# A slot earlier for the gates of the first recurrence, and its freed slot inside the tail of that recurrence

## The reference

```
h = rmsnorm(x, norm_mix_pre)
proj = h @ w_in                      # gq gk gv gg1 gr | pu | mq mk mv | gates
logit = gg1 @ w_g2 + b_g             # the recurrence's gate
log_a = log_sigmoid(logit) / 16
bc = cumsum(log_a) over time         # chunked in the reference, one scan in the kernel
attn[t,s] = sum_d q[t,d] k[s,d] exp(bc[t,d]-bc[s,d]),  s <= t
o = attn @ v ;  o = rmsnorm(o) * norm_w * silu(r)        # -> branch a
yb = pool_mixer(pu) ; yc = moba_mixer(mq, mk, mv)        # moba: 8 heads of causal softmax attention
mixed = s0 * (ya @ Wa) + s1 * (yb @ Wb) + s2 * (yc @ Wc) ; x = x + rmsnorm(mixed @ w_out)
```

## Time and profile before

| | before |
|---|---|
| median of 3 runs | 1155.04 us (1150.1 to 1155.22) |
| the profiled execution | 1149.21 us |
| its span, first to last instruction | 1147.0 us |
| mean granted PE clock in it | 0.996 |
| PE / ACT / DVE busy | 97% / 53% / 65% |

### The profile page before, as it was taken

How to read it: one execution, slowest core, us unless ns; L and a number is a source line. 1 busy time by engine, 2 the same in 40 slices (tenths; PEclk the granted TensorE clock), 3 DMA queues, 4 the chain that set the end, 5 groups by cost and what they waited for, 6 DMA issues and landing times.

```text
span 1147.0 us, 22790 instructions
## 1 busy us (share of the span) xinstructions
PE 1108.8 (97%) x9528; PEld 1053.9 (92%) x9528; DVE 750.1 (65%) x975; ACT 608.0 (53%) x788; POOL 0.2 (0%) x4
## 2 busy tenths in 40 slices
PE   7999999999999999999999999979999999999997
PEld 7999999989999998999999999979998989999997
DVE  6355667676555555688879565665557666777776
ACT  5364555346444444677566544366454546554554
POOL 0000000000000000000000000000000000000000
PEclk9999999999999999999999999999999999999999
DMA  7533435454555454344434434333444554555540
GB/s 261 215 109 114 149 146 185 177 189 158 184 184 185 183 187 177 111 147 153 180 111 152 147 145 147 110 112 131 164 150 149 209 191 151 186 197 183 183 183 37
DMA packets 27111, 184.40 MB, mean 161 GB/s; under 512 B 3080, under 2 KB 3608, under 8 KB 5400
## 3 DMA queue, kind: packets, MB, share of 16 engines
q1 hardware_dynamic: 26456, 181.38, 43.8%
q10 hardware_dynamic: 576, 1.85, 0.5%
HBM read 182.17 MB, written 1.05 MB: 160 GB/s over the span
## 4 chain that ended last, share of the span: by engine, by line
PE 78%; DVE 11%; ACT 8%; issue 2%; DMA 0%; ACTq 0%; SPq 0%; DVEq 0%
PE pp L303 55%; DVE wlo L285 5%; ACT whi L278 4%; PE pm L1653 3%; PE pm L1654 3%; PE pm L1655 3%; PE pm L883 1%; PE pm L384 1%; PE pm L386 1%; PE pm L385 1%; PE pm L757 1%; ACT XH L732 1%; PE pm L723 1%; PE pm L891 1%; PE pm L1502 1%
## 5 line engine op out<-in xcount | busy, mean ns | idle before, releaser
L285 DVE TENSOR_TENSOR wlo<-raw,whi 128x2048 fp32r<-128x2048 f32 x169 | 386.4, 2291 | 215.0 <-ACT whi L278 210.9
L303 PE MATMUL pp<-XH,whi 128*128 128x256 f32 x1696 | 485.7, 286 | 7.6 <-DVE wlo L285 6.1
L303 PE MATMUL pp<-XL,whi 128*128 128x256 f32 x1696 | 480.5, 283 | 0.0
L303 PE MATMUL pp<-XH,wlo 128*128 128x256 f32 x1696 | 480.5, 283 | 0.0
L278 ACT ACTIVATE whi<-raw 128x2048 fp32r<-128x2048 f32 x169 | 321.6, 1909 | 48.8 <-PE pp L303 31.7
L303 PEld LDWEIGHTS pp<-XH,whi 128*128 128x128 f32 x1696 | 325.8, 192 | 14.7 <-issue 7.8
L303 PEld LDWEIGHTS pp<-XL,whi 128*128 128x128 f32 x1696 | 325.9, 192 | 0.8
L303 PEld LDWEIGHTS pp<-XH,wlo 128*128 128x128 f32 x1696 | 325.8, 192 | 0.0
L1707 ACT ACTIVATE Y<-P 128x256 fp32r<-128x256 f32 x44 | 18.4, 418 | 132.6 <-DVE P L1740 132.6
L303 PE MATMUL pp<-Y,whi 128*128 128x256 f32 x480 | 86.9, 283 | 0.0
L303 PEld LDWEIGHTS pp<-Y,whi 128*128 128x128 f32 x480 | 75.2, 192 | 0.0
(11 more groups left out here) (308 smaller groups left out, 1303.3 us busy)
## 6 DMA issues: line engine op xcount, KB each, us to landing
raw<-stream SPq DMA_DIRECT2D x169, 1024.0 KB, 4.8
P<-gains ACTq DMA_DIRECT2D x3, 512.0 KB, 3.5
X<-xt SPq DMA_DIRECT2D x2, 512.0 KB, 4.4
raw<-stream SPq DMA_DIRECT2D x2, 512.0 KB, 6.8
out<-P SPq DMA_DIRECT2D x4, 256.0 KB, 2.2
C<-consts SPq DMA_DIRECT2D x1, 345.5 KB, 11.6
P<-rows_w ACTq DMA_DIRECT2D x1, 272.0 KB, 2.7
U<-poolw SPq DMA_DIRECT2D x1, 256.0 KB, 10.5
```

The source lines that it names most:

```text
L285: dve.tensor_tensor(wlo[:, slot, :], raw[:, slot, :], whi[:, slot, :].bitcast(F32), ALU.subtract).then_inc(lo_ready, 1)
L303: done = pe.matmul(dst, a, b, start=first and n == 0, stop=last and n == 2, **kw)
```

## The change

The two logit matmuls become a function of their own and stand on PE behind slot 2; the gates stand on ACT and DVE inside the opening's slots. PE's slot in front of S0 is gone, so from S0 on every set of scores has one slot fewer behind it. The slot that is freed stands in front of the value products, and a slot that belonged to MOBA (14) stands between the sums and the spread: GLA now has slots 6 to 14, MOBA 15 to 25. ACT and DVE get one more `st.go(1)` in the tail of GLA. MOBA's first `st.go(1)` goes from PE and stays on ACT and DVE. ACT's three rounding copies of constants (1861 to 1863) move from the start of GLA to its end.

```diff
--- before.py
+++ after.py
@@ -103,7 +103,7 @@
 
 
 
-W_GLA, W_MOBA, W_BRANCH, W_OUT = (6, 8), (14, 12), (26, 6), (32, 4)
+W_GLA, W_MOBA, W_BRANCH, W_OUT = (6, 9), (15, 11), (26, 6), (32, 4)
 W_START = (0, 6)
 W_HGRN, W_MLSTM, W_SSD, W_BRANCH2, W_OUT2 = (
     (BLK2 + first, n) for first, n in ((0, 27), (27, 13), (40, 20), (60, 4), (64, 4)))
@@ -842,15 +842,17 @@
         else:
             eng.wait_ge(S("scores_masked"), 6 * r + FINE.index(n) + 1)
 
+    def gated_logits_pe(pe):
+
+        pe.wait_ge(S("g1_copied"), 1)
+        for t in range(2):
+            i = pe.matmul(bank(3)[:, t * 256:t * 256 + 256], G2W[:, t * 128:t * 128 + 128], SM[0:16, 0:256], start=True, stop=True)
+        i.then_inc(S("logit_ready"), 1)
+
     def gated_pe(pe, r, st):
         g = gated(r)
-        if r == 0:
-            pe.wait_ge(S("g1_copied"), 1)
-            for t in range(2):
-                i = pe.matmul(bank(3)[:, t * 256:t * 256 + 256], G2W[:, t * 128:t * 128 + 128], SM[0:16, 0:256], start=True, stop=True)
-            i.then_inc(S("logit_ready"), 1)
         for n in range(9):
-            st.go(1 if n in LEVEL_SLOTS[r] or r == n == 0 else 0)
+            st.go(1 if n in LEVEL_SLOTS[r] else 0)
             if n == 0:
                 pe.wait_ge(S("gated_inputs_ready"), r + 1)
             else:
@@ -883,6 +885,7 @@
                         i = pe.matmul(fine_scores(r, n)[b:b + 32, slot, u, :], lhs[rows, tile, at + b:at + b + 32],
                                       rhs[rows, tile, t:t + 32], start=True, stop=True)
             i.then_inc(S("scores_ready"), 1)
+        st.go(1 if r == 0 else 0)
         taken_scores(pe, r, 3)
         pe.wait_ge(S("diagonal_spread"), 4 * r + 4)
         wait_evac(pe, VALUES[r])
@@ -1785,14 +1790,15 @@
         for k in range(KT):
             i = pe.matmul(bank(4)[0:16, 0:256], G1W[:, k * 16:k * 16 + 16], HF[:, k, :], start=k == 0, stop=k == KT - 1)
         i.then_inc(S("g1_ready"), 1)
+        st.go(1)
+        gated_logits_pe(pe)
         st.finish()
         st.window(*W_GLA)
-        wait_evac(pe, W_GLA[0] - 1)
+        wait_evac(pe, 1)
         gated_pe(pe, 0, st)
         st.finish()
         st.window(*W_MOBA)
-        st.go(1)
-        wait_evac(pe, W_MOBA[0] - 1)
+        wait_evac(pe, W_MOBA[0] - 2)
         pe.wait_ge(S("tables_loaded"), 16)
         moba_pe(pe, st)
         st.finish()
@@ -1852,18 +1858,20 @@
         st.go(3)
         act.wait_ge(S("g1_ready"), 1)
         act.activation(SM[0:16, 0:256], bank(4)[0:16, 0:256], ACT.Copy).then_inc(S("g1_copied"), 1)
+        st.go(1)
+        gated_logits_act(act)
+        st.go(1)
+        gated_log_act(act, 0)
         st.finish()
         st.window(*W_GLA)
         wait_evac(act, W_GLA[0] - 1)
+        gated_act(act, 0, st)
 
         act.wait_ge(S("tables_loaded"), 16)
         act.wait_ge(S("masks_loaded"), 16)
         act.activation(CR[:, 0:128], C[:, CIDENT:CIDENT + 128], ACT.Copy).then_inc(S("masks_rounded"), 1)
         act.activation(CR[:, 128:256], P[:, MASKS, 0:128], ACT.Copy).then_inc(S("masks_rounded"), 1)
         act.activation(CR[:, 256:276], C[:, CSEL:CSEL + 20], ACT.Copy).then_inc(S("masks_rounded"), 1)
-        gated_logits_act(act)
-        gated_log_act(act, 0)
-        gated_act(act, 0, st)
         st.finish()
         st.window(*W_MOBA)
         wait_evac(act, W_MOBA[0] - 1)
@@ -1950,12 +1958,14 @@
         split_lo(dve, 1, 1)
         keep_dve(dve, "norm_mix_pre")
         st.window(*W_START)
+        st.go(4)
+        gated_gates_dve(dve, 0)
+        st.go(1)
+        gated_decay_dve(dve, 0, slice(0, 2))
         st.finish()
         st.window(*W_GLA)
-        wait_evac(dve, W_GLA[0] - 1)
+        wait_evac(dve, 1)
         dve.wait_ge(S("tables_loaded"), 16)
-        gated_gates_dve(dve, 0)
-        gated_decay_dve(dve, 0, slice(0, 2))
         gated_dve(dve, 0, st)
         st.finish()
         st.window(*W_MOBA)
```

## The result

The changed kernel takes 1154.62 us (median of 20 runs, 1152.78 to 1156.25), the kernel before in the same series 1151.02 us (20 runs). The ratio, taken over all runs, is 1.0025, with a 95% interval from 1.0016 to 1.0034: 0.25% slower, 2.9 us (the two medians lie 3.6 us apart). Timed again beside other kernels (first experiment of the second series) it is 1.0023 [1.0010, 1.0037]. The forecast was +0.7 us, no difference that can be told; with more runs than its bound of 0.5% assumed, it can be told, and it is a loss.

The account below looks back on a forecast made before the run. PE looked binding, but ACT and DVE were taken to pace MOBA once their lead is gone. GLA -4.02 - 1.35, MOBA -0.64 + 6.6: 0.6 to 0.7 us later, 1155.04 + 0.7 = 1155.7 us; range 1149.5 to 1159.0.

Parts of the forecast that it names:

- third rival: PE's clock falls in the value products and behind the wait at T(0): +3.7 us, median 1158.7; chance 0.14.
- Waits of GLA: PE's four waits before logits (0.69), S0 (1.14), value products (1.53) and spread (0.66) all go: -4.02 us.
- 1.53 goes: Slot 12 in front of GLA's value products covers PE's wait there, saving 1.53 us.
- the spread's end: PE ends GLA's spread at 121.1 us, with slot 14 done before it; before the change it ended at 120.72.
- The clock in the value products: With dense matmuls in front, PE's clock stays at 1.00 in GLA's value products, saving 1.35 us.
- The start of MOBA's chain: Copies (0.61) and table load (1.28) add to the 13.72 us from DVE's product to head 0's probabilities, p(0).
- The wait of T(0): PE waits 3.2 us for p(0) before MOBA's head 0 transposes, asking at 133.6 when it is ready at 136.8.
- T(6): PE waits about 1.3 us before MOBA's head 6 transposes, which come at 181.6 us against 180.90 before.
- T(2) and T(4): PE waits about 1.2 and 0.9 us before the transposes of MOBA's heads 2 and 4.
- A single fall at T(0) is absorbed: One clock fall behind the T(0) wait, costing PE 1.35 to 1.7 us, is absorbed by waits at T(2) and T(4).
- T(7): MOBA's head 7 transposes come near 188.7 us; the forecast falls if before 186 or after 191.
- The first rival: MOBA's rounds run faster when started late, so GLA's gain is kept: -5.4 us, median 1149.7; chance 0.13.

Follow-up runs that it names:

- first experiment of the second series: The changed kernel, unedited, timed again beside the other kernels of that series: 1153.79 us against 1150.96 for the kernel before, ratio 1.0023.
- e7: From e4, six idle matmuls (0.96 us in all) put on PE in front of slot 12: 1150.09 us, ratio 0.9984 to the kernel before.
- e5: From e1, slot 12 also given back to the attention stage, none in front of the value products: 1147.66 us, ratio 0.9980 to the kernel before.
- e2: Changed kernel with ACT's three copies and table load moved in front of its wait for the norm product: 1150.89 us, ratio 0.9991 to the kernel before.
- e3: Changed kernel with 24 idle matmuls filling PE's wait in front of T(0): 1153.16 us, ratio 1.0009 to the kernel before.
- e4: Changed kernel with the edits of e1 and e2 together: 1147.92 us, ratio 0.9967 to the kernel before.
- e6: From e4, the attention's first scores moved into the gap between sums and spread: 1147.14 us, ratio 0.9971 to the kernel before.
- e1: Changed kernel with slot 14 put back in front of the attention's first scores: 1148.56 us, ratio 0.9965 to the kernel before.

## Why the prediction was right, and where it was off

The range (1149.5 to 1159.0) holds 1154.62, and the sign was right. How near the time came is in part luck: the forecast stood on a median of three runs, 1155.04, and the kernel before has 1151.02 over 20. In the difference, which is what was worked out, it is +0.7 forecast and +2.9 measured, inside the bounds of the rivals (-5.4 to +3.7) but over the forecast's own (-0.6 to +2.1) and nearer to the third rival's +3.7. The steps:
- Waits of GLA: three went as worked out, 0.69, 1.14 and 0.66. The fourth is the step that failed, "1.53 goes": it went in name, and 1.26 us of stall came inside the slot that covers it. The term is worth 0.27. It puts the spread's end at 121.73 and not at 121.1; a start 0.2 us earlier and value products 0.3 us shorter make up for part of it. (The terms of the forecast add up to 120.93, not 121.1, a slip of 0.2.) No row of the kernel before shows the stall; there PE waits 1.53 us at that point. Why it comes is open (e7).
- The clock in the value products: right, 1.00, and 0.66 us for a head instead of 1.18. That the dense slot in front is the reason is not shown: in e5 they ran at 1.00 without it, behind a wait of 1.53 us.
- The start of MOBA's chain: right to 0.04 us (15.65 against 15.61), and e2 shows that copies and load are what was added. The load at 124.60 ends at 125.88 and the next instruction starts at 125.90. The drain of 1.38 us that the Trainium skill adds to a load ("ScalarE: Activation LUTs", What ACT_TABLE_LOAD costs) would have given 17.0, an estimate from that page. These rows show none.
- The wait of T(0): 3.19 for 3.2. T(6) 1.18 for 1.3. T(2) and T(4) did not wait, as PE came late to them.
- "A single fall at T(0) is absorbed": nearly. Half of the third rival's mechanism was there, the fall at T(0) but not the one in the value products, with 2.8 us of PE lost in place of 1.35 to 1.7, and for once ACT's split stood 0.66 us for PE. The split's wait is what it cost: in the second profile the fall behind T(0) is shorter, no split waits, and p(0) to p(6) is 44.69 us, as in e3 without a fall, against 45.46 here. e3 bounds the cost at T(7) by 0.6 us.
- Sum: T(7) forecast 188.7, came at 190.08, 1.4 later: 0.6 from the later spread, 0.75 from the chain's longer way to p(6). At 189.75 in the second profile it is 1.1, all of it from the later start (p(0) at 137.86). Balance in the first block +2.0 instead of +0.7.
- Of the measured +2.9 us the first block explains 1.7 to 2.0 by the two profiles. The rest, under 1 us, is within what the falls of the clock elsewhere do to a run, and is not settled.
- The first rival had nearly the right size for what could have been had, though not for this kernel: with slot 14 left where it was, 4.0 us of the 5.4 are kept.

## What to carry to other kernels

A slot used to cover a short wait of one engine is taken from the engines behind it as lead: ask where the next stage goes at the pace of another chain, and whether that chain starts later by the slot. Here 0.66 us were covered at a price of 4.3 us at T(7) (e4 against e2), and the rest of the change (gates early, one slot in front of the value products) is worth 4 us together once that slot is left in place. Look also at what else the edit puts between the event that starts such a chain and its first step: two microseconds of work stood there, with six idle ones just in front.

## What the runs showed of the hardware that I had not expected

- PE stops for 1.1 to 1.4 us inside slot 12, 22 matmuls after the last block of 128 small ones (each with its load, in 1.4 us), in seven of seven profiles of kernels with that order; it is marked "issue". The same block one set earlier is followed by no stop, so the block alone is not the cause.
- A load of ACT's table takes 1.28 us and the next instruction starts 0.01 to 0.02 us behind it (125.88 and 125.90 in the changed kernel, 118.92 and 118.93 in e2).
- The length of a wait does not settle whether the clock falls at it, and two profiles of one kernel can differ. At the 3.1 us wait near 770 us it stayed at 1.00 in the kernel before, e4 and e6 and fell in the other seven profiles. At the 2.1 us wait near 250 us it fell in e1, e2, e4, e5, e6 and the changed kernel's first profile, and stayed in the kernel before, e3, e7 and its second. At the 2.1 us wait near 495 us, with sixteen matmuls of 4 and 16 columns right behind it, it fell in all ten. A fall near 250 us cost 1.5 to 1.6 us to the next mark, one near 770 us 1.3 to 2.7. So two single profiles may differ by some microseconds for no reason of the change; a difference is read at marks near the change, not from the spans.
